# Gate and up products of 32 feed-forward chunks by Strassen's scheme, seven half-size products instead of eight

## The chip, the cores and the metric

The kernel runs on one core of a Trainium2 chip. The metric is the device time of one execution in microseconds (us).

## The reference

`reference()` runs one first block (three mixing branches and an MLP) and then two layers of a second block on x of 512 tokens by 1024 features, all in fp32. Each layer of the second block holds two gated feed-forward blocks with 2816 hidden features, four in all; the change is in these:

```
def swiglu(x, w_gate, w_up, w_down):
    return (jax.nn.silu(x @ w_gate) * (x @ w_up)) @ w_down
...
for l in range(DEPTH_2):
    x = x + 0.5 * swiglu(rms_norm_2(x, ffn1_norm[l]), ffn1_w_gate[l], ffn1_w_up[l], ffn1_w_down[l])
    ...
    x = x + 0.5 * swiglu(rms_norm_2(x, ffn2_norm[l]), ffn2_w_gate[l], ffn2_w_up[l], ffn2_w_down[l])
```

## The kernel before

Activations lie transposed: features on the 128 partitions, the 512 tokens along the free dimension. An fp32 product is made of three TensorE matmuls on fp32r operands (`mm3`, L492): every weight and every activation is kept as a rounded part `_hi` and a remainder `_lo`, and `mm3` adds w_lo x x_hi, w_hi x x_lo and w_hi x x_hi in one PSUM bank.

The weights come as a stream of units of 128x1024 numbers (512 KB) in the order in which TensorE uses them. A unit passes four engines, each with a ring of three slots: SyncE loads it into `raw` when GpSimd has finished the slot's last unit (L408), ScalarE rounds it into `w_hi` (`round_unit`, called by `tick` once TensorE is through with the tile before, two units ahead), GpSimd subtracts in four pieces into `w_lo` (L485), and TensorE waits for `lo_ready` (L500).

A feed-forward block is cut into 11 chunks of 256 hidden features. A chunk is two gate tiles and two up tiles of 128 features by 512 tokens (`project`, 8 x 3 matmuls of 512 columns each, a unit each) and eight down tiles (`down`, 2 x 3 matmuls each, four tiles to a unit). The down tiles of a chunk come after the gate and up tiles of the next one. Gate tiles go to PSUM banks 0 and 1, up and down tiles to a ring of four banks.

The operand of the gate and up tiles is x times the norm's gain; 1/rms of each token (`rt`) is multiplied in afterwards. VectorE scales each gate and up tile by `rt` (L1845, L2273), ScalarE takes silu of the gate, VectorE multiplies gate and up (L2277) and splits the hidden tile (L2240, L2242, in `hidden`), and adds each down tile to the residual `xres` (L2204). In the first block of each layer `layer_columns` (L2409 to L2423) forms some columns for later. Each engine runs its own program; what orders them are the semaphores named in the code.

## Time and profile before

| | |
|---|---|
| median of 3 runs | 3382.36 us (3381.77 to 3383.36) |
| the profiled execution | 3382.04 us, of it 3380.3 us span |
| TensorE | 99% of the span busy, 15438 matmuls |
| VectorE, ScalarE, GpSimd | 50%, 39%, 53% of the span busy |
| granted TensorE clock, mean | 0.999 |

The span runs from the first to the last instruction on the device; the execution's own time has some 1.7 us around it. Busy shares are means over the whole program. Matmuls are pipelined and overlap in the records, so the time of one is read from start to start.

### The profile page before, as it was taken

The numbers are of one execution on the slowest core, as the hardware profiler recorded it, in microseconds if no ns is written. First come the engines' busy times: TensorE is split into PE (matmuls) and PEld (weight loads), VectorE is DVE, ScalarE is ACT, GpSimd is POOL, SyncE is SP. The second block draws the span as 40 slices with busy tenths as digits, with TensorE's granted clock in tenths as the row PEclk, the third lists the DMA queues.
The fourth block names the chain that finished last, engine by engine and source line by source line (L and its number), as shares of the span: only waits on it lengthen the run. The fifth ranks groups of instructions, "written<-read, shape, count | busy, mean of one in ns | idle before, by whom it ended". The sixth has DMA issues, their size and how long they took to land.

```text
span 3380.3 us, 46752 instructions
## 1 busy us (share of the span) xinstructions
PE 3363.0 (99%) x15438; PEld 2740.0 (81%) x15438; DVE 1695.4 (50%) x2673; ACT 1313.9 (39%) x1817; POOL 1801.0 (53%) x2316
## 2 busy tenths in 40 slices
PE   9999999999999999999999999999999999999999
PEld 5888777888888887888888888888887888888887
DVE  8887785544553438614434434544358334243444
ACT  4365664222232226735633222322237545532222
POOL 6444445655555555553455555555556543465554
PEclk9999999999999999999999999999999999999999
DMA  6212552322222323331223222222223222222223
GB/s 224 86 67 69 175 168 100 114 94 99 93 100 94 99 93 101 99 125 63 69 100 102 100 93 99 94 100 93 99 93 112 88 100 75 81 95 98 99 93 112
DMA packets 94459, 343.03 MB, mean 101 GB/s; under 512 B 10609, under 2 KB 11249, under 8 KB 93954
## 3 DMA queue, kind: packets, MB, share of 16 engines
q1 hardware_dynamic: 86978, 312.11, 27.4%
q10 hardware_dynamic: 7360, 29.29, 2.7%
q8 instruction: 78, 1.28, 0.2%
q14 instruction: 43, 0.35, 0.0%
HBM read 335.03 MB, written 2.13 MB: 100 GB/s over the span
## 4 chain that ended last, share of the span: by engine, by line
PE 78%; issue 10%; POOL 7%; DVE 2%; DVEq 1%; ACT 1%; DMA 0%; ACTq 0%; POOLq 0%; SPq 0%
PE ps L494 24%; PE ps L496 24%; PE ps L495 24%; POOL w_lo L485 7%; PE ps L986 1%; PE ps L968 1%; PE ps L660 1%; PE ps L661 1%; PE ps L662 1%; DVE arena L2301 0%; PE ps L977 0%; DVEq L2303 0%; PE ps L626 0%; POOL xres L463 0%; DVE arena L1857 0%
## 5 line engine op out<-in xcount | busy, mean ns | idle before, releaser
L485 POOL TENSOR_TENSOR w_lo<-raw,w_hi 128x256 fp32r<-128x256 f32 x2256 | 1776.6, 818 | 1557.1 <-ACT w_hi L1074 1557.0
L1074 ACT ACTIVATE w_hi<-raw 128x1024 fp32r<-128x1024 f32 x566 | 595.9, 1055 | 1025.9 <-PE ps L496 1007.8
L494 PE MATMUL ps<-a_hi,w_lo 128*128 128x512 f32 x2208 | 873.6, 396 | 0.3 <-DVE a_lo L1803 0.3
L496 PE MATMUL ps<-a_hi,w_hi 128*128 128x512 f32 x2208 | 860.7, 390 | 0.0
L495 PE MATMUL ps<-a_lo,w_hi 128*128 128x512 f32 x2208 | 859.9, 389 | 0.0
L494 PE MATMUL ps<-b_hi,w_lo 128*128 128x512 f32 x2112 | 823.9, 390 | 4.2 <-DVE b_lo L1875 4.0
L495 PE MATMUL ps<-b_lo,w_hi 128*128 128x512 f32 x2112 | 822.5, 389 | 0.0
L496 PE MATMUL ps<-b_hi,w_hi 128*128 128x512 f32 x2112 | 822.4, 389 | 0.0
L494 PEld LDWEIGHTS ps<-a_hi,w_lo 128*128 128x128 f32 x2208 | 414.8, 188 | 100.3 <-issue 16.9
L496 PEld LDWEIGHTS ps<-a_hi,w_hi 128*128 128x128 f32 x2208 | 414.4, 188 | 87.8
L495 PEld LDWEIGHTS ps<-a_lo,w_hi 128*128 128x128 f32 x2208 | 414.9, 188 | 82.6 <-issue 0.5
L494 PEld LDWEIGHTS ps<-b_hi,w_lo 128*128 128x128 f32 x2112 | 396.9, 188 | 89.4 <-issue 6.6
L496 PEld LDWEIGHTS ps<-b_hi,w_hi 128*128 128x128 f32 x2112 | 396.9, 188 | 83.1
L495 PEld LDWEIGHTS ps<-b_lo,w_hi 128*128 128x128 f32 x2112 | 396.8, 188 | 81.6
L2204 DVE SCALAR_TENSOR_TENSOR xres<-ps,xres 128x512 f32<-128x512 f32 x368 | 246.8, 689 | 174.9 <-PE ps L496 165.7
L1845 DVE TENSOR_TENSOR ps<-ps,arena 128x512 f32<-128x512 f32 x96 | 66.3, 699 | 392.0 <-PE ps L496 362.2
L2273 DVE TENSOR_TENSOR ps<-ps,arena 128x512 f32<-128x512 f32 x88 | 61.6, 700 | 282.3 <-PE ps L496 281.9
L1092 ACT ACTIVATE sgate<-ps 128x512 f32<-128x512 f32 x88 | 52.1, 597 | 358.3 <-DVE ps L1845 358.2
L2204 DVE SCALAR_TENSOR_TENSOR xres<-ps,cols,xres 128x512 f32<-128x512 f32 x136 | 99.1, 748 | 65.8 <-PE ps L496 53.7
L2242 DVE TENSOR_TENSOR a_lo<-arena,a_hi 128x512 fp32r<-128x512 f32 x120 | 126.0, 1050 | 9.8 <-issue 1.2
L660 PE MATMUL ps<-w_lo,a_hi 128*128 128x256 f32 x320 | 93.4, 292 | 0.0
L662 PE MATMUL ps<-w_hi,a_hi 128*128 128x256 f32 x320 | 90.4, 283 | 0.0
(286 smaller groups left out, 2772.3 us busy)
## 6 DMA issues: line engine op xcount, KB each, us to landing
raw<-in_stream SPq DMA_DIRECT2D x567, 512.0 KB, 3.3
arena<-in_mod_w ACTq DMA_DIRECT2D x32, 512.0 KB, 4.2
arena<-in_mod_w SPq DMA_DIRECT2D x16, 512.0 KB, 11.5
arena<-arena ACTq DMA_DIRECT2D x16, 256.0 KB, 3.6
arena<-cum_rows ACTq DMA_DIRECT2D x2, 2048.0 KB, 8.0
xres<-in_x_t SPq DMA_DIRECT2D x4, 512.0 KB, 5.1
arena<-in_first SPq DMA_DIRECT2D x8, 256.0 KB, 11.7
xres<-in_x_t ACTq DMA_DIRECT2D x1, 2048.0 KB, 9.5
```

Source lines behind the costliest of these rows:

```text
L485: last = pool.tensor_tensor(w_lo[:, s, part], raw[:, s, part], w_hi[:, s, part].bitcast(F32), ALU.subtract)
L494: pe.matmul(out, lo, x_hi, start=start, stop=False)
L495: pe.matmul(out, hi, x_lo, start=False, stop=False)
L496: return pe.matmul(out, hi, x_hi, start=False, stop=stop)
L660: pe.matmul(out, a_hi[:, f, tok], w_lo[:, s, w], start=f == 0, stop=False)
L662: last = pe.matmul(out, a_hi[:, f, tok], w_hi[:, s, w], start=False, stop=f == KT - 1)
L1074: act.activation(w_hi[:, slot, :], raw[:, slot, :], ACT.Copy).then_inc(hi_ready, 1)
L1092: act.activation(out, ps[:, c.act.n % 2, :], func, bias=bias).then_inc(act_evacuated, 1)
L1845: dve.tensor_tensor(bank, bank, rt, ALU.mult).then_inc(tile_scaled, 1)
L2204: dve.scalar_tensor_tensor(xres[:, m, :], y, scale, xres[:, m, :], ALU.mult, ALU.add).then_inc(dve_evacuated, 1)
L2242: dve.tensor_tensor(a_lo[:, n, :], t, a_hi[:, n, :].bitcast(F32), ALU.subtract).then_inc(hidden_ready, 1)
L2273: dve.tensor_tensor(y, y, rt, ALU.mult)
```

## The change

Of each block's 11 chunks the first three (`PLAIN`) stay as they are, eight (`FAST`) are made anew. In these the gate pair is one product of a 256x1024 weight matrix with 1024x512 activations, cut in halves every way (features out 2 x 128, features in 2 x 512, tokens 2 x 256). Strassen's scheme (in Winograd's form) makes it of seven products of a 128x512 with a 512x256 block instead of eight; each is 4 x 3 matmuls of 256 columns (`fast_product`). The up pair likewise. So a chunk has 14 products, 168 matmuls of 256 columns, in place of 96 of 512. The down tiles are unchanged.

What the scheme adds:

- Activations: once per block, VectorE forms the normalised x (`normalise_x`), its low parts and four combinations of its quarters (`make_turns`), ScalarE rounds them (`round_xn`, `round_turns`), GpSimd makes the combinations' low parts (`low_turns`). All this stands beside the plain chunks 1 and 2. The fast chunks' tiles need no scaling by `rt`.
- Weights: each chunk still loads six units, but rounds and splits nine: VectorE makes four sums of 128x512 for the gate pair and four for the up pair (`sums`), which fill three further units (unit 2: gate, 5: up, 6: both). Units 0 to 2 carry the gate products, 3 to 5 the up products, 6 the last of both, 7 and 8 the down tiles. ScalarE may not round a unit before its sums are written: unit 4 waits for two up sums, units 5 and 6 for all four.
- Results: VectorE joins the products in PSUM by 5 + 2 operations of 128x256 for each pair (`combine`, `combine_last`), after ScalarE has copied the first product aside (`copy_first`).

VectorE's order in a fast chunk is: combine gate, three gate sums for the next chunk, combine up, last combinations, a fourth gate sum, eight down tiles, two hidden tiles, four up sums for the next chunk. SyncE and GpSimd get run lists that change between plain and fast parts.

The diff, cut to its core:

```diff
+PLAIN = 3
+FAST = FFN_CHUNKS - PLAIN
+GROUP, FAST_UNITS, FAST_TILES = 6, 9, 22
+TOK = S // 2
...
+        def fast_raw(part):
+            base = ENDS[part] % RING
+            return fast_own + [raw[:, (base + j) % RING, :] for j in range(3)]
+        def fast_units(part):
+            g1, g2, u1, u2, d1, d2 = fast_raw(part)
+            return [g1, g2, gate_s23, u1, u2, up_s23, both_s4, d1, d2]
...
+                    sp.dma_start(to[j], stream[at + j]).then_inc(fast_loaded[j], 16)
+                with sp.Fori(1, FAST) as i:
+                    for j, unit in enumerate((2, 2, 5, 5, 7, 8)):
+                        sp.wait_ge(fast_lo, i * FAST_UNITS + (done - FAST_UNITS + unit + 1))
+                        sp.dma_start(to[j], stream[bass.ds(i * GROUP + (at + j), 1)].rearrange("o p n -> p (o n)")
+                                     ).then_inc(fast_loaded[j], 16)
...
+                with pool.Fori(0, FAST) as i:
+                    for j, of in enumerate(fast_units(part)):
+                        s = (end + j) % RING
+                        pool.wait_ge(fast_hi, i * FAST_UNITS + (part * FAST * FAST_UNITS + j + 1))
+                        low(w_lo[:, s, :], of, w_hi[:, s, :]).then_inc(fast_lo, 1)
...
+            def fast_product(out, j, half, operand):
+                pe.wait_ge(fast_lo, c.fast_lo.at(j + 1))
+                s = (c.units.n + j) % RING
+                for k in range(4):
+                    w = slice(half * 4 * P + k * P, half * 4 * P + k * P + P)
+                    x_hi, x_lo = operand(k)
+                    last = mm3(out, w_hi[:, s, w], w_lo[:, s, w], x_hi, x_lo, k == 0, k == 3)
+                last.then_inc(fast_done, 1)
...
+                    fast_product(ps[:, x, left], j, 0, x_1a)
+                    free(-2, -3)
+                    fast_product(ps[:, z, left], j, 1, x_2a)
+                    free(-1, -1)
+                    fast_product(ps[:, y, right], j + 1, 0, t_1)
+                    fast_product(ps[:, y, left], j + 1, 1, t_4)
+                    fast_product(ps[:, z, right], j + 2, 0, t_2)
+                    free(0, 0)
+                    fast_product(ps[:, w, left], j + 2, 1, t_3)
+                for half, banks in enumerate((gate_banks, UP_BANKS)):
+                    pe.wait_ge(first_copied, c.gate_silu.at(1 + half))
+                    fast_product(ps[:, banks[0], right], 6, half, x_2b)
+                pe.wait_ge(hidden_ready, c.hid.at(2))
...
+            def fast_round(j, chunk):
+                raw_at = {0: 0, 1: 1, 3: 2, 4: 3, 7: 4, 8: 5}
+                if j in raw_at:
+                    act.wait_ge(fast_loaded[raw_at[j]], c.fast_raw.at(16 * chunk + 16))
+                if j in (1, 2, 6):
+                    act.wait_ge(gate_summed, c.gate_sums.at(4 * chunk + {1: 2, 2: 4, 6: 4}[j]))
+                if j in (4, 5, 6):
+                    act.wait_ge(up_summed, c.up_sums.at(4 * chunk + {4: 2, 5: 4, 6: 4}[j]))
+                slot = (ENDS[c.part.n] + j) % RING
+                act.activation(w_hi[:, slot, :], fast_units(c.part.n)[j], ACT.Copy).then_inc(fast_hi, 1)
+            def fast_silu(m):
+                bank = fast_banks(c.part.n)[2 * m]
+                act.wait_ge(gate_ready, c.gate_ready.at(2 - m))
+                act.activation(sgate[:, m, :], ps[:, bank, :], ACT.Silu).then_inc(gate_silu, 1)
+                table[0] = "evicted"
+            def copy_first(bank, to):
+                act.activation(to, ps[:, bank, 0:TOK], ACT.Copy).then_inc(first_copied, 1)
+            def fast_chunk(last):
+                for j in range(3, FAST_UNITS):
+                    act.wait_ge(fast_done, c.fast.at(2 * (j - 2)))
+                    fast_round(j, 0)
+                    if j == 4:
+                        act.wait_ge(hidden_ready, c.hid.at(0))
+                        copy_first(fast_banks(c.part.n)[0], gate_m1)
+                    if j == 6:
+                        fast_silu(1)
+                        copy_first(UP_BANKS[0], up_m1)
+                fast_silu(0)
+                for j, tiles in enumerate((14, 18, 22)):
+                    act.wait_ge(fast_done, c.fast.at(tiles))
+                    if not last:
...
+                def first_chunk(m):
+                    round_xn(2 * m)
+                    round_xn(2 * m + 1)
+                gate_tiles(True, first_chunk)
...
+                gate_tiles(True, lambda m: round_turns(1 + m))
+                tick()
+                round_turns(3)
...
+            def normalise_x(g, k):
+                for i in range(2):
+                    last = dve.scalar_tensor_tensor(x_turns[k][:, i * S:i * S + S], xres[:, 4 * i + k, :], par(PAR2, g, 4 * i + k), rt,
+                                                    ALU.mult, ALU.mult)
+                last.then_inc(xn_ready, 1)
+            def make_turns(k):
+                x_1a, x_1b, x_2a, x_2b = (x_turns[k][:, i * TOK:i * TOK + TOK] for i in range(4))
+                dve.wait_ge(xn_rounded, 4 * c.part.n + k + 1)
+                dve.tensor_tensor(q11_lo[:, k, :], x_1a, q11_hi[:, k, :].bitcast(F32), ALU.subtract)
+                dve.tensor_tensor(a_lo[:, 4 + k, :], x_turns[k][:, S:2 * S], a_hi[:, 4 + k, :].bitcast(F32), ALU.subtract)
+                dve.drain()
+                dve.tensor_tensor(x_1a, x_1b, x_1a, ALU.subtract)
+                dve.drain()
+                dve.tensor_tensor(x_1b, x_2b, x_1b, ALU.subtract)
+                dve.drain()
+                dve.tensor_tensor(x_2b, x_2b, x_1a, ALU.subtract)
+                dve.drain()
+                dve.tensor_tensor(x_2a, x_2a, x_2b, ALU.subtract).then_inc(turns_made, 1)
+            def sums(kind, first, end, chunk):
+                gate = kind == "gate"
+                raws = fast_raw(c.part.n)
+                one, two = raws[0:2] if gate else raws[2:4]
+                s23, s4 = (gate_s23, both_s4[:, 0:S]) if gate else (up_s23, both_s4[:, S:2 * S])
+                summed = gate_summed if gate else up_summed
+                for n in range(first, end):
+                    dve.drain()
+                    if n == 0:
+                        for j in (0, 1) if gate else (2, 3):
+                            dve.wait_ge(fast_loaded[j], c.fast_raw.at(16 * chunk + 16))
+                        if chunk:
+                            dve.wait_ge(fast_lo, c.fast_lo.at(3 if gate else 6))
+                        dve.tensor_tensor(s23[:, S:2 * S], one[:, 0:S], two[:, 0:S], ALU.subtract).then_inc(summed, 1)
+                    if n == 1:
+                        dve.tensor_tensor(two[:, 0:S], two[:, 0:S], two[:, S:2 * S], ALU.add).then_inc(summed, 1)
+                    if n == 2:
+                        dve.tensor_tensor(s23[:, 0:S], two[:, 0:S], one[:, 0:S], ALU.subtract).then_inc(summed, 1)
+                    if n == 3:
+                        if chunk:
+                            dve.wait_ge(fast_lo, c.fast_lo.at(7))
+                        dve.tensor_tensor(s4, one[:, S:2 * S], s23[:, 0:S], ALU.subtract).then_inc(summed, 1)
...
+            def combine(banks, tiles, copied, m1, u4):
+                x, z, y, w = blocks(banks)
+                dve.wait_ge(first_copied, c.gate_silu.at(copied))
+                dve.wait_ge(fast_done, c.fast.at(tiles))
+                dve.tensor_tensor(sum_u2, m1, z[1], ALU.add)
+                dve.drain()
+                dve.tensor_tensor(sum_u3, sum_u2, w[0], ALU.add)
+                dve.tensor_tensor(u4, sum_u2, y[1], ALU.add)
+                dve.drain()
+                dve.tensor_tensor(y[0], sum_u3, y[0], ALU.add)
+                return dve.tensor_tensor(y[1], sum_u3, y[1], ALU.add)
...
+            def combine_last(banks, tiles, m1, u4):
+                x, z = blocks(banks)[0:2]
+                dve.drain()
+                dve.wait_ge(fast_done, c.fast.at(tiles))
+                dve.tensor_tensor(x[0], m1, z[0], ALU.add)
+                return dve.tensor_tensor(x[1], u4, x[1], ALU.add)
...
+            def fast_hidden(half, m):
+                if m == 0:
+                    dve.wait_ge(gate_silu, c.gate_silu.at(2))
+                t = tt[:, m, :]
+                dve.tensor_tensor(t, sgate[:, m, :], ps[:, UP_BANKS[2 * m], :], ALU.mult).then_inc(up_read, 1)
+                hidden(half, m, t)
+            def fast_chunk(last):
+                gate_banks = fast_banks(c.part.n)
+                assert (c.dve.n + c.dve.shift) % WIDE == FAST_BANK[c.part.n]
+                combine(gate_banks, 6, 1, gate_m1, gate_u4).then_inc(gate_ready, 1)
+                if not last:
+                    sums("gate", 0, 3, 1)
+                combine(UP_BANKS, 12, 2, up_m1, up_u4)
+                combine_last(gate_banks, 13, gate_m1, gate_u4).then_inc(gate_ready, 1)
+                combine_last(UP_BANKS, 14, up_m1, up_u4)
+                if not last:
+                    sums("gate", 3, 4, 1)
+                for m in range(8):
+                    fast_down(m)
+                    if last and m in (1, 4):
                         dve.drain()
-                        add_tiles(ffn_out)
+                        fast_hidden(1, m // 4)
...
+            def ffn_chunks(g):
+                def first_beside(n):
+                    if n == 0:
+                        normalise_x(g, 2)
+                        normalise_x(g, 3)
+                    if n == 1:
+                        make_turns(0)
+                normalise_x(g, 0)
+                normalise_x(g, 1)
+                ffn_up(1, first_beside)
+                dve.drain()
+                add_tiles(ffn_out)
+                make_turns(1)
+                def second_beside(n):
+                    if n < 2:
+                        make_turns(2 + n)
+                    if n == 2:
+                        dve.wait_ge(turns_ready, 4 * c.part.n + 1)
+                        sums("gate", 0, 2, 0)
+                    if n == 3:
+                        sums("gate", 2, 3, 0)
+                ffn_up(0, second_beside)
+                dve.drain()
+                add_tiles(ffn_out)
                 dve.memset(cols[:, 126:127], 0.0).then_inc(normalised, 1)
...
+                dve.drain()
+                with loop(dve, FAST - 1, c, fast=FAST_TILES, fast_raw=16, fast_lo=FAST_UNITS, gate_silu=2):
+                    fast_chunk(False)
+                fast_chunk(True)
```

Where the order of instructions changes: the first place is VectorE at the end of a chunk. Before, in a turn of its loop, a hidden tile follows its up tile; `arena` in the first row is `rt`.

```order
L2273 TENSOR_TENSOR ps<-ps,arena 128x512 [waits tiles_done]
L2275 ISA
L2277 TENSOR_TENSOR arena<-sgate,ps 128x512 [waits act_evacuated]
L2240 CAST a_hi<-arena 128x512
L2242 TENSOR_TENSOR a_lo<-arena,a_hi 128x512
```

Now, with the last down tile in the first row; `arena` and `raw` in L2634 to L2642 are weight units and their sums.

```order
L2673 SCALAR_TENSOR_TENSOR xres<-ps,xres 128x512 [waits fast_done]
L2680 TENSOR_TENSOR arena<-sgate,ps 128x512 [waits gate_silu]
L2555 CAST a_hi<-arena 128x512
L2557 TENSOR_TENSOR a_lo<-arena,a_hi 128x512
L2680 TENSOR_TENSOR arena<-sgate,ps 128x512
L2555 CAST a_hi<-arena 128x512
L2557 TENSOR_TENSOR a_lo<-arena,a_hi 128x512
L2633 REGISTER_ALU [waits fast_loaded3,fast_loaded2]
L2634 TENSOR_TENSOR arena<-arena,raw 128x512 [waits fast_lo]
L2636 TENSOR_TENSOR raw<-raw 128x512
L2638 TENSOR_TENSOR arena<-raw,arena 128x512
L2642 TENSOR_TENSOR arena<-arena 128x512 [waits fast_lo]
```

The two hidden tiles have moved behind all eight down tiles, and four sums, each with both inputs in SBUF, stand behind them.

The second place is ScalarE in a fast chunk, from the rounding of unit 3 on. Before, a rounding waited for a load and a tile alone:

```order
L1073 REGISTER_ALU [waits tiles_done]
L1074 ACTIVATE w_hi<-raw 128x1024 [waits raw_loaded0]
L1091 REGISTER_ALU [waits dve_evacuated]
L1092 ACTIVATE sgate<-ps 128x512 [waits tile_scaled]
L187 REGISTER_ALU
L1074 ACTIVATE w_hi<-raw 128x1024 [waits raw_loaded1,tiles_done]
L187 REGISTER_ALU
L1074 ACTIVATE w_hi<-raw 128x1024 [waits raw_loaded2,tiles_done]
```

Now:

```order
L1785 ACTIVATE w_hi<-arena 128x1024 [waits fast_loaded2]
L1800 REGISTER_ALU
L1783 ISA [waits fast_loaded3,fast_done]
L1785 ACTIVATE w_hi<-raw 128x1024 [waits up_summed]
L1803 ISA
L1795 ACTIVATE arena<-ps 128x256 [waits hidden_ready]
L1800 REGISTER_ALU
L1783 REGISTER_ALU [waits fast_done]
L1785 ACTIVATE w_hi<-arena 128x1024 [waits up_summed]
L1800 REGISTER_ALU
L1785 ACTIVATE w_hi<-arena 128x1024 [waits up_summed,gate_summed,fast_done]
```

The second, third and fourth rounding (units 4, 5 and 6) now wait for VectorE's sums, and every later rounding stands behind them in ScalarE's queue.

## Rows read from the trace of the kernel before

**Rows 1.** The page: busy us (share of span) x instructions; costliest groups.
```profile
PE 3363.0 (99%) x15438; PEld 2740.0 (81%) x15438; DVE 1695.4 (50%) x2673; ACT 1313.9 (39%) x1817; POOL 1801.0 (53%) x2316
...
L485 POOL TENSOR_TENSOR w_lo<-raw,w_hi 128x256 fp32r<-128x256 f32 x2256 | 1776.6, 818 | 1557.1 <-ACT w_hi L1074 1557.0
```

**Rows 2.** Windows of 100 us in a feed-forward block.
```profile
core 0: us, PE busy (x) PEld busy (x) DVE busy (x) ACT busy (x) POOL busy (x), PEclk, DMA share, GB/s
1900.00:2000.00 100.00, 100.00 (x443) 82.83 (x442) 38.74 (x55) 22.02 (x24) 56.70 (x75) 1.00 0.28 95
2000.00:2100.00 100.00, 100.00 (x443) 82.84 (x442) 39.16 (x56) 23.07 (x25) 54.72 (x73) 1.00 0.29 97
```

**Rows 3.** Timeline of TensorE there: start us, us, engine line op.
```profile
2000.41 0.39 PE L496 MATMUL ps<-b_hi,w_hi 128*128 128x512 f32 x1
2000.64 0.39 PE L494 MATMUL ps<-a_hi,w_lo 128*128 128x512 f32 x1
```

**Rows 4.** Timeline of VectorE there; in brackets idle time and who ended it.
```profile
2000.84 0.70 DVE L2273 TENSOR_TENSOR ps<-ps,arena 128x512 f32<-128x512 f32 x1 [2.13 <-PE ps L496]
2001.69 0.69 DVE L2277 TENSOR_TENSOR arena<-sgate,ps 128x512 f32<-128x512 f32 x1
2002.46 0.53 DVE L2240 CAST a_hi<-arena 128x512 fp32r<-128x512 f32 x1
2003.07 1.07 DVE L2242 TENSOR_TENSOR a_lo<-arena,a_hi 128x512 fp32r<-128x512 f32 x1
...
2017.16 0.70 DVE L1845 TENSOR_TENSOR ps<-ps,arena 128x512 f32<-128x512 f32 x1 [4.75 <-PE ps L496]
2022.60 0.70 DVE L1845 TENSOR_TENSOR ps<-ps,arena 128x512 f32<-128x512 f32 x1 [4.74 <-PE ps L496]
```

**Rows 5.** Timeline of GpSimd there.
```profile
2001.98 3.47 POOL L485 TENSOR_TENSOR w_lo<-raw,w_hi 128x256 fp32r<-128x256 f32 x4 [1.98 <-ACT w_hi L1074]
2007.50 2.83 POOL L485 TENSOR_TENSOR w_lo<-raw,w_hi 128x256 fp32r<-128x256 f32 x4 [2.05 <-ACT w_hi L1074]
2012.94 2.82 POOL L485 TENSOR_TENSOR w_lo<-raw,w_hi 128x256 fp32r<-128x256 f32 x4 [2.61 <-ACT w_hi L1074]
```

**Rows 6.** Timeline of TensorE in the first block, matmuls of 256 columns.
```profile
157.43 0.28 PE L660 MATMUL ps<-w_lo,a_hi 128*128 128x256 f32 x1
...
159.83 0.28 PE L662 MATMUL ps<-w_hi,a_hi 128*128 128x256 f32 x1
```

**Rows 7.** Groups of VectorE by shape, whole span: busy us, mean ns, idle before.
```profile
L2164 DVE SCALAR_TENSOR_TENSOR arena<-ps,arena 128x256 f32<-128x256 f32 x8 | 3.4, 425 | 2.2 <-ACT arena L1368 1.6
```

**Rows 8.** Two lines of VectorE, whole span: ns min/median/max of one.
```profile
L2204 DVE SCALAR_TENSOR_TENSOR xres<-ps,xres x368: 676/691/694, 977.5 to 3377.1; 128x512 f32<-128x512 f32 x184
...
L2242 DVE TENSOR_TENSOR a_lo<-arena,a_hi x120: 692/1069/1073, 593.0 to 3357.6; 128x512 fp32r<-128x512 f32 x120
```

**Rows 9.** Timelines of GpSimd and VectorE where both are dense.
```profile
2532.89 8.84 POOL L485 TENSOR_TENSOR w_lo<-raw,w_hi 128x256 fp32r<-128x256 f32 x8 [2.30 <-ACT w_hi L1074]
...
2532.36 6.47 DVE L2301 SCALAR_TENSOR_TENSOR arena<-arena,params 128x512 f32<-128x512 f32 x6
2538.75 1.22 DVE L1857 SCALAR_TENSOR_TENSOR arena<-xres,params,arena 128x512 f32<-128x512 f32 x1
2539.90 1.22 DVE L1803 TENSOR_TENSOR a_lo<-arena,a_hi 128x512 fp32r<-128x512 f32 x1
```

**Rows 10.** Timeline of ScalarE in the feed-forward block.
```profile
2000.84 1.06 ACT L1074 ACTIVATE w_hi<-raw 128x1024 fp32r<-128x1024 f32 x1 [4.38 <-PE ps L496]
```

**Rows 11.** Timeline of TensorE at its one wait for GpSimd.
```profile
591.37 0.39 PE L496 MATMUL ps<-b_hi,w_hi 128*128 128x512 f32 x1
591.92 0.50 PE L494 MATMUL ps<-b_hi,w_lo 128*128 128x512 f32 x1 [0.16 <-POOL w_lo L485]
592.25 0.39 PE L495 MATMUL ps<-b_lo,w_hi 128*128 128x512 f32 x1
```

**Rows 12.** Timeline of VectorE at the head of the first feed-forward block.
```profile
952.17 0.70 DVE L2273 TENSOR_TENSOR ps<-ps,arena 128x512 f32<-128x512 f32 x1 [2.08 <-PE ps L496]
...
954.48 1.07 DVE L2242 TENSOR_TENSOR a_lo<-arena,a_hi 128x512 fp32r<-128x512 f32 x1
...
958.43 0.16 DVE L2423 TENSOR_SCALAR cols<-cols 128x8 f32<-128x8 f32 x1
```

**Rows 13.** The page, DMA issues: KB each, us to landing.
```profile
raw<-in_stream SPq DMA_DIRECT2D x567, 512.0 KB, 3.3
```

More of the change, by code:

```diff
@@ new lines, in low_run @@
+            def low_run(first, end):
+                n = first
+                while n < end:
+                    turns = (end - n) // RING
+                    if n % RING == 0 and turns:
+                        with pool.Fori(n // RING, n // RING + turns) as i:
+                            for s in range(RING):
+                                pool.wait_ge(hi_ready, i * RING + (s + 1))
+                                low(w_lo[:, s, :], raw[:, s, :], w_hi[:, s, :]).then_inc(lo_ready, 1)
+                        n += turns * RING
+                    else:
+                        s = n % RING
+                        pool.wait_ge(hi_ready, n + 1)
+                        low(w_lo[:, s, :], raw[:, s, :], w_hi[:, s, :]).then_inc(lo_ready, 1)
+                        n += 1
@@ L910, in ffn @@
                 project(bank_v(), of=OF_B)
-                with loop(pe, FFN_CHUNKS // 2, c, units=12, tiles=24, act=4, dve=20, hid=4):
+                for chunk in range(1, PLAIN):
                     up()
-                    down(0)
-                    up()
-                    down(1)
-                down(0)
-                c.dve.ring = 2
+                    down((chunk - 1) % 2)
+                c.part.n += 1
+                pe.wait_ge(turns_ready, 4 * c.part.n)
+                fast_chunk(True)
```

269 lines of the change are left out of this document (231 added, 38 removed).

## The prediction, made before the changed kernel ran

> **What bounds the kernel now.** I read the page first: TensorE has work in 99% of the span, GpSimd in 53% [rows 1]. The windows of 100 us inside a feed-forward block then show TensorE at 100%, 443 matmuls in each, clock granted in full, VectorE at 39%, ScalarE at 22%, GpSimd at 57% [rows 2]. The timeline of TensorE shows a new 512-column matmul every 0.227 us and no wait between tiles [rows 3]. VectorE's scaling of one tile and of the next start 5.44 us apart, which is 24 matmuls of 0.2267 us, and it is idle before them, waiting for TensorE [rows 4]. GpSimd takes 2.82 us for a weight unit and then sits idle about 2 us until ScalarE has rounded the next one [rows 5]. So TensorE's stream of columns is the bound, and the others wait for it. A chunk costs 144 matmuls, 144 x 0.2267 = 32.64 us.
>
> **The half-size products.** The trace has this shape: in the first block, 256-column matmuls start at 157.43 and at 159.83 us with 19 between, 0.120 us apart [rows 6]. A unit of 1024 weight columns feeds two products of 12 such matmuls, 24 x 0.120 = 2.88 us. A fast chunk is then seven units of 2.88 (20.16 us) and two down units of 24 x 0.2267 = 5.44 us (10.88), 31.04 us in all. Against 32.64 that is 1.60 us less, and 32 such chunks (8 in each of 4 blocks) would give 51 us back, if TensorE stays the bound. The Trainium skill ("TensorE: Matmul & The Clock Gate", section on the gap between matmuls) gives N/2.4 ns plus 2.5 ns, 109 ns for 256 columns. The row has 120, and 227 where the rule has 216, so the measurement decides. By the rule's 109 ns TensorE's seven units would be 1.8 us shorter per chunk, 58 us more over 32 chunks, if nothing else bound.
>
> **What the others must do for it.** A fast chunk has 9 units to round and to split instead of 6: three are weight sums that VectorE writes. GpSimd needs 9 x 2.82 = 25.4 us per 31.04 us, where it needed 16.9 per 32.64. VectorE makes 8 sums of 128x512 with both inputs in SBUF, and 14 combinations of 128x256 with one input in PSUM. The nearest row for the latter is 0.425 us [rows 7]. It loses the four scalings of 0.70 us.
>
> The two engines do not run such work side by side. Where VectorE has one PSUM input its time does not move (L2204: 676 to 694 ns), but the subtraction of two SBUF tiles, L2242, spreads from 692 to 1073 ns [rows 8]. On the same stretch the GpSimd unit beside one cast and one such subtraction took 3.47 us instead of 2.82 [rows 4, 5]. Where both are dense, eight GpSimd instructions took 8.84 us instead of 2 x 2.82 = 5.64, while VectorE's two-SBUF operations took 1.08 to 1.22 us each [rows 9]: each such operation costs GpSimd 3.20/8 = 0.40 us and itself about 0.38. The Trainium skill ("SBUF — State Buffer", who interferes with whom) states that a VectorE instruction with two SBUF inputs and a GpSimd one that reads SBUF exclude each other for the whole instruction. The rows agree, and this rule speaks against the change. In total GpSimd would need 25.4 + 8 x 0.40 + 2 x 0.65 = 29.9 us of 31.04: not the bound by its sum. But the weight ring has three slots, so it cannot work ahead, and what counts is the order inside the chunk.
>
> **One fast chunk, walked.** Time 0 is TensorE's end of a chunk's eighth down tile; unit k of the next chunk is due at 2.88k.
> - VectorE starts 0.20 after a tile ends (2000.64 to 2000.84, [rows 3, 4]), and adds the tile in 0.69 [rows 8]: 0.89.
> - Two hidden tiles (product, cast, subtraction), 2001.69 to 2004.14 = 2.45 each [rows 4], with some 0.1 between: 6.0. Before the change nothing near waited for this.
> - The first two up sums, at 1.07 plus 0.08 for the drain each, as L2242 has it beside GpSimd [rows 4]: 8.3. ScalarE's rounding of unit 4 waits for them (L1783 to L1785), and units 5 to 8 stand behind it in its queue.
> - ScalarE 1.06, GpSimd 0.08 behind it [rows 5, 10]: GpSimd starts unit 4 at 9.5. Beside it run the last sums, one of them in full: 2.82 + 0.40, done at 12.7. TensorE wanted it at 11.52.
> - VectorE is through the up sums at 10.6, combines the gate products (5 operations of about 0.42, L2653 to L2659) to 12.7 and goes into three sums for the next chunk. Beside them GpSimd's unit 5 takes 2.82 + 3 x 0.40 = 4.0: done at 16.75.
> - TensorE restarts 0.1 to 0.2 late: after its one wait for GpSimd the next matmul starts 0.33 behind the first instead of 0.227 [rows 11]. It starts unit 5 at 16.9, where 5 x 2.88 = 14.40 was due.
>
> Behind that point GpSimd keeps up: units 6 to 8 see VectorE on PSUM inputs, and the two down units are 10.88 us long. So a chunk lasts 31.04 + 2.5 = 33.5 us. Register operations ahead of waits are not in the walk (the gap between L2273 and L2277 is 0.15 where a drain alone leaves 0.08, [rows 4]), and I take 33.7. That is 1.06 more than 32.64, and 34 us over 32 chunks. The first and the last chunk of a block go much the same: in the first, unit 2 waits for a gate sum that now stands behind the last additions (some 1.2 us), in the last, the hidden tiles lie between the additions.
>
> **Entry of each block.** Normalising x (8 operations), the 16 differences and 8 low parts go beside plain chunks 1 and 2, which have the time (VectorE 39% busy). In the two blocks where VectorE also forms per-layer columns (954.48 + 1.07 to 958.6, [rows 12]), ScalarE's second tick of plain chunk 1 stands behind two normalised tiles. From chunk 1's start at 951.97 (the scaling at 952.17 less 0.20): columns done 6.6, four normalisings at 1.1 to 11.1, ScalarE's rest to 12.7, rounding to 13.8, GpSimd 2.82 + 4 x 0.40 to 18.3, and TensorE wants that unit at 3 x 5.44 = 16.3. I add 2 us for each of these two blocks, 4 in all; nothing for the other two, where it comes 3.1 us earlier. The turned inputs' low parts (16 GpSimd instructions, 11.3 us per block) lie in its 45% of idle time. Loads: 6 units a chunk as before, 3.3 us from issue to landing [rows 13], and each is asked for more than 5 us ahead: nothing. If a load came late, its whole lateness would reach TensorE.
>
> **Sum.** The profiled execution took 3382.0 us (3380.3 span and 1.7 around it), the median 3382.4. 3382 + 34 + 4 = 3420 us, 1.1% slower.
>
> **Rivals.**
> - *The port costs nothing on the path, faster.* If sums and units pass each other, unit 5 is on time, the chunk lasts 31.04, and 3382 - 51 + 4 = 3335 us. It decides at 16.0 us in the walk: 0.9 less than I have makes the chunk as long as before. For it: GpSimd's sum of 29.9 us fits. Against it: four two-SBUF operations stand in a row ahead of unit 4, and I have read their price twice. Chance 0.18, with all that ends between. A further 0.06 for a chunk at 32.64 within 0.2 us.
> - *GpSimd stays behind, slower still.* If units 6 to 8 too take 3.3 us, 0.4 above the 2.88 of TensorE, 1.2 us more a chunk: 3420 + 38 = 3458 us. For it: at unit 5 there is no idle time of GpSimd left. Against: its neighbours on VectorE then have PSUM inputs. Chance 0.12.
> - *The entry stalls in all four blocks*, about 8 us each where I have 1 on average: 3448 us. VectorE's extra work there is some 31 us in 65 (20 wide two-SBUF operations at 1.1, 20 of 256 columns at about 0.45). Chance 0.04.
>
> **How the numbers follow.** Forecast 0.60. Its own range is 3395 to 3445: a contended operation at 0.35 or 0.45 us instead of 0.40, and 0.3 us of waits per chunk either way. Bounds: an up sum at 0.69 (no contention) or 1.22 (the longest row), so 2 x 0.38 less or 2 x 0.15 more; combinations at 0.3 or 0.6. The range 3360 to 3460 reaches into the first rival and takes in the second. A measurement tells about 0.2% (7 us) from no change: faster 0.18, same 0.06, slower 0.76.
>
> **What would show it.** In a window in the fast part: TensorE below 100%, its idle time ended by w_lo on GpSimd ahead of 256-column matmuls, two or three times a chunk, the longest ahead of units 4 and 5; a chunk of 33.7 us; GpSimd near 90%; sums near 1.1 us, combinations near 0.4; ScalarE waiting for VectorE's raw sum ahead of unit 4. A chunk of 31.1 us, or GpSimd units at 2.9 us beside the sums, would make me wrong; so would 256-column matmuls that do not start 0.120 us apart, or waits for a DMA.

## The result and the profile after

The changed kernel takes 3443.4 us, median of four runs from 3439.3 to 3455.5, against 3382.5 us: ratio 1.0186, interval 1.016 to 1.0212. It is 61 us slower. The profiled execution was the fastest of the four, 3439.31 us with a span of 3437.6, against 3382.04 and 3380.3 before. The runs are now 16 us apart; before the change they were 1.6 us apart.

The page's busy line, and two groups of its costliest:

```profile
PE 3337.1 (97%) x17742; PEld 2805.1 (82%) x17742; DVE 2158.1 (63%) x3377; ACT 1466.4 (43%) x2025; POOL 2221.6 (65%) x2764
...
L634 PE MATMUL ps<-a_hi,w_lo 128*128 128x512 f32 (+1 forms) x2720 | 1023.1, 376 | 21.7 <-DVE xres L2673 14.2
...
L588 POOL TENSOR_TENSOR w_lo<-arena,w_hi 128x256 fp32r<-128x256 f32 x768 | 642.2, 869 | 124.7 <-ACT w_hi L1785 124.7
```

The windows that answer to [rows 2], now filled with fast chunks:

```profile
1900.00:2000.00 100.00, 91.73 (x626) 83.99 (x625) 68.23 (x101) 32.88 (x39) 84.56 (x105) 0.98 0.27 95
2000.00:2100.00 100.00, 93.68 (x643) 85.85 (x642) 71.80 (x108) 33.00 (x39) 87.61 (x107) 1.00 0.25 90
```

TensorE idles 6 to 8% of a stretch in which it never idled before. Its timeline in one fast chunk, which began at 1119.69 us, cut to the rows with a wait in brackets:

```profile
1128.94 0.39 PE L634 MATMUL ps<-q_hi,w_lo 128*128 128x256 f32 x1 [0.59 <-POOL w_lo L588]
1132.80 0.39 PE L634 MATMUL ps<-t_hi,w_lo 128*128 128x256 f32 x1 [0.74 <-POOL w_lo L588]
1136.47 0.39 PE L634 MATMUL ps<-t_hi,w_lo 128*128 128x256 f32 x1 [0.59 <-POOL w_lo L588]
```

These are the first matmuls of units 3, 4 and 5, at 9.25, 13.11 and 16.78 us of the chunk, where 8.64, 11.52 and 14.40 were due. Each waits for GpSimd's low part. VectorE and GpSimd in that chunk:

```profile
1126.25 0.90 DVE L2634 TENSOR_TENSOR arena<-arena,raw 128x512 f32<-128x512 f32 x1 [0.25 <-issue]
1127.25 1.06 DVE L2636 TENSOR_TENSOR raw<-raw 128x512 f32<-128x512 f32 x1
1128.40 1.04 DVE L2638 TENSOR_TENSOR arena<-raw,arena 128x512 f32<-128x512 f32 x1
```

```profile
1129.48 3.27 POOL L588 TENSOR_TENSOR w_lo<-raw,w_hi 128x256 fp32r<-128x256 f32 x4 [0.59 <-ACT w_hi L1785]
1132.70 6.96 POOL L588 TENSOR_TENSOR w_lo<-arena,w_hi 128x256 fp32r<-128x256 f32 x8
```

A sum takes 1.04 to 1.06 us beside GpSimd, and the eight GpSimd instructions of units 5 and 6 take 6.96 us instead of 2 x 2.82 [rows 5]. Inner fast chunks follow each other at 33.89 us (median of the starts of unit 0; a plain chunk is 32.64).

Two chunks of the first block, one of the second and one of the fourth are 2.3 to 3.9 us longer still. VectorE in one of them:

```profile
1211.02 0.42 DVE L2667 TENSOR_TENSOR ps<-arena,ps 128x256 f32<-128x256 f32 x1
1211.59 4.76 DVE L2642 TENSOR_TENSOR arena<-arena 128x512 f32<-128x512 f32 x1
1216.27 2.47 DVE L2673 SCALAR_TENSOR_TENSOR xres<-ps,xres 128x512 f32<-128x512 f32 x4
```

GpSimd and TensorE at the same place:

```profile
1207.41 5.62 POOL L588 TENSOR_TENSOR w_lo<-raw,w_hi 128x256 fp32r<-128x256 f32 x8
1212.97 2.82 POOL L588 TENSOR_TENSOR w_lo<-arena,w_hi 128x256 fp32r<-128x256 f32 x4
1217.36 2.81 POOL L588 TENSOR_TENSOR w_lo<-arena,w_hi 128x256 fp32r<-128x256 f32 x4 [1.56 <-ACT w_hi L1785]
```

```profile
1218.28 0.49 PE L634 MATMUL ps<-a_hi,w_lo 128*128 128x512 f32 x1 [2.17 <-DVE xres L2673]
```

The fourth gate sum (L2642), elsewhere 1.23 us, takes 4.76: it is done only after GpSimd's unbroken run has ended at 1215.79. GpSimd's twelve instructions from 1207.41 on take their undisturbed 0.70 us each. Four additions of down tiles queue behind the sum, and TensorE, which wants their banks, stands still for 2.17 us. I call this a shut-out. The trace has four (L2642 at 1211.6, 1248.0, 1923.7 and 3173.6).

**Where the 57.3 us of span went**, from the starts of TensorE's units: inner chunks 24 x 1.25 = 30.0; the first fast chunk of each block 4 x (33.39 - 32.64) = 3.0; the last 4 x (34.51 - 32.64) = 7.5; shut-outs 11.2 (two of 2.48, one of 3.93, one of 2.34); the rest is 5.6, of which some 5.4 are the entries of the blocks.

### The profile page after: what moved, and what is told of

It reads as the page before. It is cut to its first block, busy times and chain, and to the rows that moved or that the text cites. A ratio compares the mean times of both kernels' runs of the same rounds, so it can differ in the third digit from the quotient of the medians.

```text
span 3437.6 us, 53314 instructions
## 1 busy us (share of the span) xinstructions
PE 3337.1 (97%) x17742; PEld 2805.1 (82%) x17742; DVE 2158.1 (63%) x3377; ACT 1466.4 (43%) x2025; POOL 2221.6 (65%) x2764
## 4 chain that ended last, share of the span: by engine, by line
POOL 41%; PE 31%; issue 22%; DVE 3%; ACT 2%; DVEq 1%; POOLq 0%; ACTq 0%; DMA 0%; SPq 0%
POOL w_lo L588 39%; PE ps L634 8%; PE ps L636 8%; PE ps L635 8%; POOL t_lo L588 1%; PE ps L1217 1%; PE ps L1199 1%; PE ps L801 1%; PE ps L802 1%; PE ps L803 1%; DVE arena L2761 0%; PE ps L1208 0%; DVEq L2763 0%; ACT w_hi L1305 0%; DVE arena L2172 0%
## 5 line engine op out<-in xcount | busy, mean ns | idle before, releaser
L634 PE MATMUL ps<-a_hi,w_lo 128*128 128x512 f32 (+1 forms) x2720 | 1023.1, 376 | 21.7 <-DVE xres L2673 14.2
L636 PE MATMUL ps<-a_hi,w_hi 128*128 128x512 f32 (+1 forms) x2720 | 1006.1, 370 | 0.0
L635 PE MATMUL ps<-a_lo,w_hi 128*128 128x512 f32 (+1 forms) x2720 | 1005.6, 370 | 0.0
L588 POOL TENSOR_TENSOR w_lo<-arena,w_hi 128x256 fp32r<-128x256 f32 x768 | 642.2, 869 | 124.7 <-ACT w_hi L1785 124.7
L634 PE MATMUL ps<-b_hi,w_lo 128*128 128x512 f32 x1088 | 425.9, 391 | 4.7 <-DVE b_lo L2190 4.0
L635 PE MATMUL ps<-b_lo,w_hi 128*128 128x512 f32 x1088 | 424.0, 390 | 0.0
L636 PE MATMUL ps<-b_hi,w_hi 128*128 128x512 f32 x1088 | 423.9, 390 | 0.0
L634 PE MATMUL ps<-t_hi,w_lo 128*128 128x256 f32 x1024 | 292.8, 286 | 44.1 <-POOL w_lo L588 44.1
L636 PE MATMUL ps<-t_hi,w_hi 128*128 128x256 f32 x1024 | 286.9, 280 | 0.0
L635 PE MATMUL ps<-t_lo,w_hi 128*128 128x256 f32 x1024 | 285.4, 279 | 0.0
```

Source lines behind the costliest of these rows:

```text
L588: last = pool.tensor_tensor(to[:, at], of[:, at], hi[:, at].bitcast(F32), ALU.subtract)
L634: pe.matmul(out, lo, x_hi, start=start, stop=False)
L635: pe.matmul(out, hi, x_lo, start=False, stop=False)
L636: return pe.matmul(out, hi, x_hi, start=False, stop=stop)
```

## The experiments

VectorE's instructions in a fast chunk are written below as sg0 to sg3 (gate sums), su0 to su3 (up sums), cg, cu (combinations), lg, lu (last combinations), d0 to d7 (additions of down tiles), h0, h1 (hidden tiles). The changed kernel has `cg sg0 sg1 sg2 cu lg lu sg3 d0..d7 h0 h1 su0..su3`. Kernels 1, 2 and 8 were run once, the others four to ten times.

**1. Sums with one input.** The eight sums become copies of 128x512, so the weights' sums are left out. With the second input the instruction changes too: TENSOR_REDUCE in place of TENSOR_TENSOR.

```diff
+            def one_input(to, of):
+                one = lambda v: v.rearrange("p (n o) -> p n o", o=1)
+                return dve.tensor_reduce(to, one(of), mybir.AxisListType.X, ALU.add)
-                        dve.tensor_tensor(s23[:, S:2 * S], one[:, 0:S], two[:, 0:S], ALU.subtract).then_inc(summed, 1)
+                        one_input(s23[:, S:2 * S], one[:, 0:S]).then_inc(summed, 1)
```

> All eight weight sums of a fast chunk are written by an operation of the same 512 columns with one SBUF input instead of two (the sums' values are wrong by this, so the result is not the reference's). Theory A, VectorE's two-input operations and GpSimd exclude each other: the sums take 0.6 to 0.7 us each, GpSimd's units beside them 2.8 us, unit 4 is late by 0.3 us and unit 5 not at all, a chunk lasts 31.3 us and the run 3347 us. Theory B, what counts is that the up sums stand behind the hidden tiles in VectorE's order: only the sums' own time shrinks, 0.38 us for each of two on the path, a chunk lasts 33.1 us and the run about 3410 us. Theory C, a ring of three slots cannot carry nine units per chunk whatever VectorE does: the chunk stays at 33.9 us and the run near 3440 us.

Measured: 3354.6 us, inner chunks of 31.57 us. VectorE's timeline there, three sums in one row, and GpSimd's beside them:

```profile
1187.85 2.24 DVE L2623 TENSOR_REDUCE arena<-arena 128x512 f32<-128x512 f32 x3 [0.33 <-issue]
```

```profile
1187.14 5.62 POOL L588 TENSOR_TENSOR w_lo<-arena,w_hi 128x256 fp32r<-128x256 f32 x8
```

The same number of instructions of the same width, at the same places, no longer lengthen GpSimd's: 5.62 us for the eight that took 6.96. What the two-input sums do to GpSimd costs 2.3 us in an inner chunk, and with it go the shut-outs: 3443.4 - 3354.6 = 89 us. The chunk did not reach the 31.3 us that were expected: unit 4 is still some 0.5 us late.

**2. Sums of 8 columns.** All but 8 columns of each sum are left out; the second input stays.

```diff
-                        dve.tensor_tensor(s4, one[:, S:2 * S], s23[:, 0:S], ALU.subtract).then_inc(summed, 1)
+                        dve.tensor_tensor(s4[:, 0:8], one[:, S:S + 8], s23[:, 0:8], ALU.subtract).then_inc(summed, 1)
```

> The eight sums shrink to 8 columns each (their other values stay unwritten, so the result is not the reference's); all waits and all nine units stay. Theory A: only the hidden tiles contend with GpSimd, TensorE never waits for a weight unit, a chunk lasts 31.04 us, the run 3340 us. Theory B: the path loses the sums, also about 31 us. Theory C: the chunk stays at 33.9 us, the run near 3440 us. Together with the run with one input per sum it parts the time that the sums take from what they cost through the port: A expects the two runs within 0.3 us per chunk.

Measured: 3394.1 us, far off all that was expected. The trace says why:

```profile
1138.26 3.91 DVE L2642 TENSOR_TENSOR arena<-arena 128x8 f32<-128x8 f32 x1
```

A sum of 8 columns took 3.91 us, and it did so in 27 of 28 chunks, each time ending with GpSimd's run. So the length is not the sum's own, and my first idea of the shut-out, a coin toss when a sum and a GpSimd instruction start together, fell too: this one began 0.3 us into a GpSimd instruction.

**3. Only the fourth gate sum moved**, behind d3, where GpSimd has been idle.

> Only the fourth gate sum moves, from ahead of the first down tile to behind the fourth, where GpSimd has idle time. In the changed kernel it took 4.1 to 4.8 us in four chunks of the profiled run instead of 1.3. Theory A, it is shut out by GpSimd's unbroken run of instructions by chance: no sum over 1.4 us is left, every inner chunk lasts 33.8 to 33.9 us, the run 3428 us, and the runs agree within 3 us (the changed kernel's lie 16 us apart). Rival: sums are shut out wherever GpSimd is busy: long sums come up again in other chunks, and the runs still differ by 10 us or more around 3440 us.

Measured: 3438.1 us (3427.1 to 3448.4), ratio 1.0176 (1.0158 to 1.0195). The profiled run is the one at 3427.1, and in it no sum took over 1.3 us. But the four runs lie 21 us apart, as the rival had it, and not within 3. The other three have no trace. Their mean granted clock is 0.997 to 0.998 where the traced run has 1.000, so TensorE ran at its lower level somewhere in them; what held it up is open.

**4. An order made for the 0.4 us price**: `sg0 cg cu lg sg1 sg2 sg3 d0 d1 d2 su0 d3 d4 su1 d5 su2 su3 d6 d7 lu h0 h1`.

> The same operations in another order on VectorE, inner fast chunks only: first gate sum, combine gate, combine up, last gate combination, three gate sums, then the eight down tiles with the four up sums between them (one behind the third and the fifth, two behind the sixth), last up combination, hidden tiles. Nothing is left out. Theory A: the up sums are done before the chunk ends, unit 4 no longer waits for them, and no unit meets more than one or two two-input operations: a chunk lasts 31.04 to 31.3 us, the run 3346 us, 1.1% faster than before the change. Theory B, order alone: the same direction. Theory C: the chunk stays at 33.9 us. Rival: two-input operations between the down tiles make VectorE late for the down banks, TensorE waits there, a chunk lasts 32.5 us or more and the run 3385 us or more.

Measured: 3513.4 us, ratio 1.0392 (1.0375 to 1.0409), 167 us from the forecast. The second gate sum was shut out in 26 of 28 chunks:

```profile
1154.42 5.39 DVE L2636 TENSOR_TENSOR arena<-arena 128x512 f32<-128x512 f32 x1
```

**What the traces have in common.** For each VectorE instruction with two SBUF inputs that started beside a GpSimd instruction I counted how many GpSimd had by then finished without a break, a break being idle time or an instruction that VectorE had lengthened, and how many more started before the VectorE instruction ended. Over the TENSOR_TENSOR instructions of the ten traces of the changed kernel with full-width sums, those below included: of 5,608 with a count up to 7, none had to let more than two pass. Of 110 with a count of 8 to 11, 11 had to let four or more pass. Of 55 with a count of 12 to 14, 48 did (four of the other seven met the end of GpSimd's run, three got in behind one). Another 25 had a longer run behind them: 24 met its end within two, one got in behind one. Hence the theory of the next four: a long unbroken run of GpSimd shuts VectorE out, and a break ends it. The break is made by a `drain`, one more instruction in GpSimd's program that computes nothing.

**5. The changed kernel with four GpSimd drains in a chunk.**

```diff
                         s = (end + j) % RING
+                        if j in (0, 6, 7, 8):
+                            pool.drain()
                         pool.wait_ge(fast_hi, i * FAST_UNITS + (part * FAST * FAST_UNITS + j + 1))
```

> The changed kernel with a GpSimd drain ahead of units 0, 6, 7 and 8 of each fast chunk, so that GpSimd's instructions can't overlap there; nothing else changes. Theory A: a VectorE sum is shut out only where GpSimd has run about eight or more instructions unbroken since it last idled or VectorE last broke in (in the traces so far: none of some 2,200 with seven or fewer, all that had really thirteen or more), and a drain breaks the run. Then no fourth gate sum takes over 2 us, inner chunks stay at 33.9 us, all runs lie within 5 us of each other, and the time is 3427 us (3440 less the four or five shut-outs of 2.5 to 3 us), up to 3432 for what the drains cost GpSimd. Rival B: the shut-out has to do with the sum's place behind the last combinations, or with what VectorE did before: then sums of over 4 us remain, the runs spread over 10 us and more, and the median stays at 3438 to 3445.

Measured: 3437.5 us, all four runs from 3437.3 to 3438.3, ratio 1.0165 (1.0148 to 1.0182). One sum of a first chunk was still shut out (3.35 us), none of an inner one, and the spread shrank from 16 us to 1. The drains cost more than was expected: inner chunks are 34.09 us, 0.20 longer, since GpSimd is what is late.

**6. The order of 4 with the same drains.**

> The order of e3_order (up sums between the down tiles, first gate sum ahead of the first combination, the other gate sums together) with the same four drains on GpSimd. e3_order took 3513.4 us with one sum shut out for 5.4 us in 26 of 28 chunks and inner chunks of 36.8 to 37.6 us. Theory A: the drains end the shut-outs; what is left is each sum's 0.4 us of GpSimd, now where GpSimd has time: inner chunks of 31.1 to 32.0 us, 3350 to 3370 us, below the kernel before. Rival B: shut-outs stay, 3500 us or more. Rival C: no shut-outs, but the spacing of sums between down tiles makes down banks late by itself: 33 us for a chunk and over, 3400 us and more.

Measured: 3377.5 us (3377.2 to 3378.2, ten runs), ratio 0.9986 (0.9976 to 0.9996). Same VectorE order as 3513.4 us; four drains took off 136 us. Inner chunks 32.00 us, no sum over 1.3 us. The rivals fell, the one of 4 too: with the shut-outs gone the sums between the down tiles cost no more than this. The kernel stayed 8 us above the expected band, in places that 9 and 11 take up.

**7. Another order, no drain**: `cg sg0 sg1 cu lg lu d0 d1 sg2 d2 d3 su0 sg3 d4 su1 d5 su2 d6 su3 d7 h0 h1`.

> Another order and no drain: combination, gate sums 0 and 1, the other combinations, down tiles 0 and 1, gate sum 2, tiles 2 and 3, up sum 0, gate sum 3, tile 4, up sum 1, tile 5, up sum 2, tile 6, up sum 3, tile 7, hidden tiles. Every sum behind a down tile meets GpSimd when it is idle or newly started. Theory A (shut-out after about eight unbroken instructions, 0.4 us of GpSimd for a sum that meets it): no sum over 2 us, inner chunks of 32 to 32.6 us, 3365 to 3385 us. Rival B (the price of a sum is the same wherever it stands): inner chunks stay at 33.9 us and the time at 3425 to 3440 us.

Measured: 3400.9 us (3400.7 to 3401.0), ratio 1.0055 (1.0039 to 1.0072), inner chunks 33.00 us. It is 42 us better than the changed kernel, so the place of a sum matters, and rival B fell. But I had misjudged GpSimd's idle time behind d1:

```profile
1176.43 2.10 DVE L2638 TENSOR_TENSOR arena<-arena 128x512 f32<-128x512 f32 x1
```

GpSimd's run was fourteen or fifteen instructions old here and had two to go; the sum waited for both, in all 28 chunks, and TensorE waited 31.4 us in total for the additions behind it.

**8. Sums of 8 columns with the drains.**

> e2_no_sums (sums of 8 columns for 512) with the four drains. It leaves out the sums, as e2 does. e2 took 3394.1 us, with the fourth gate sum, of 8 columns, shut out for 3.5 to 3.9 us in 27 of 28 chunks and inner chunks of 33.1 us. Theory A: without the shut-outs inner chunks are 31.1 to 31.3 us and the time 3338 to 3345 us, what was expected of e2. Rival B: 3390 us and more.

Measured: 3354.4 us. The drains took 40 us off kernel 2, but it did not reach 3345 (one 8-column sum, in a first chunk, still took 2.53 us): inner chunks are 31.61 us, with TensorE 0.35 us late at unit 4. Even an 8-column sum beside GpSimd took about 0.61 us where it takes 0.17 alone: it waits for the running instruction to end.

**9, 10. One drain, the entry and the last chunk**, on kernel 6; the second with the drain at unit 8.

```diff
-                        if j in (0, 6, 7, 8):
+                        if j == 7:
...
-                    if n == 3:
-                        sums("gate", 2, 3, 0)
...
-                add_tiles(ffn_out)
+                add_tiles(ffn_out[:4])
+                sums("gate", 2, 3, 0)
+                add_tiles(ffn_out[4:5])
+                dve.wait_ge(turns_ready, 4 * c.part.n + 3)
+                sums("gate", 3, 4, 0)
+                add_tiles(ffn_out[5:])
...
+                    dve.drain()
+                    fast_hidden(1, 0)
                     for m in range(8):
                         fast_down(m)
-                        if m in (1, 4):
+                        if m == 3:
                             dve.drain()
-                            fast_hidden(1, m // 4)
+                            fast_hidden(1, 1)
```

> e8_order_drains (3377.5 us) with three more edits. One drain, ahead of unit 7, for four: the second gate sum then meets GpSimd four or five instructions after a break. Entry: gate sum 2 goes behind the fourth addition of the last plain chunk, gate sum 3 behind the fifth, instead of ahead of the first and behind the last. Last fast chunk of a block: its hidden tiles ahead of the first down tile and behind the fourth, instead of behind the second and the fifth. Theory A: the drains gave up some 0.3 us in a chunk (inner chunks 31.6 to 31.9 us instead of 32.0), the entry gives back 0.8 us ahead of the first fast chunk and 1.5 us of the wait at 7.1 us in it, four times, and the last chunk's wait of 1.9 us falls to 0.5 us, four times: 3377.5 - 7 - 9 - 6 = 3355 us, between 3350 and 3364. Rival B: these waits are not VectorE's order but the sum of its work, and come back behind: 3370 us and more. Rival C: one drain is too few and shut-outs return: over 3380 us, with sums of over 4 us in the trace.

> As e11_entry_and_last, but the drain stands ahead of unit 8 instead of unit 7, right where the second gate sum comes. If a drain only has to lie within eight instructions of the sum, the time is that of e11_entry_and_last within 3 us. If a sum has to be lucky to fall behind it, shut-outs of 4 to 5 us return in some chunks and the time is 10 us or more above it.

Measured: 3364.1 us (ratio 0.995, 0.9936 to 0.9963) and 3364.7 us (0.9947, 0.9932 to 0.9963). The drain's place makes no difference to the median, as the theory has it. One of the first kernel's five runs took 3370.1 us, the others 3363.5 to 3364.6; it has no trace. The forecast of 3355 us was 9 us short. The last chunk fell from 32.91 to 31.48 us and the wait ahead of the first fast chunk is gone, as expected. Inner chunks are 31.88 us. But the wait at 7.1 us in the first fast chunk stayed, 1.27 us from start to start in place of 1.59, and with it most of the 6 us that I had counted for it. I had taken ScalarE's rounding of unit 2 to be held back by the gate sum; with the sum done at 1016.7 us it still starts at 1020.63, on a tile of TensorE:

```profile
1020.63 1.06 ACT L1787 ACTIVATE w_hi<-arena 128x1024 fp32r<-128x1024 f32 x1 [1.88 <-PE ps L638]
```

**11. The first up sum behind d3** instead of ahead of it, on kernel 9.

> As e11_entry_and_last, but the first up sum stands behind the addition of down tile 3 instead of ahead of it. In e8_order_drains that addition came 0.4 us late for TensorE (gap of 0.54 us at 27.8 us of the chunk). Theory A: the gap goes, 0.4 us in each of 28 chunks: up to 11 us faster than e11_entry_and_last, unless the up sums, later by 0.7 us, delay unit 4. Rival: they do, and the time is the same or above.

Measured: 3349.3 us (3348.7 to 3349.8), ratio 0.9902 (0.9886 to 0.9917). Inner chunks fell from 31.88 to 31.33 us. This version beats both kernels. Its windows of fast chunks, to be read beside the two above, and its VectorE behind the last combinations (the kernel's lines are two further down):

```profile
1900.00:2000.00 100.00, 99.67 (x676) 91.91 (x675) 73.77 (x117) 34.42 (x40) 93.03 (x116) 1.00 0.29 100
2000.00:2100.00 100.00, 99.67 (x695) 92.67 (x694) 73.92 (x117) 35.52 (x41) 91.29 (x115) 1.00 0.27 94
```

```profile
1165.55 0.42 DVE L2669 TENSOR_TENSOR ps<-arena,ps 128x256 f32<-128x256 f32 x1
1166.07 0.80 DVE L2638 TENSOR_TENSOR arena<-arena 128x512 f32<-128x512 f32 x1
1166.95 1.05 DVE L2640 TENSOR_TENSOR arena<-arena 128x512 f32<-128x512 f32 x1
```

GpSimd there, where the drain ahead of unit 7 shows as 0.23 us without work (in 31 of the 32 fast chunks):

```profile
1156.92 5.63 POOL L588 TENSOR_TENSOR w_lo<-arena,w_hi 128x256 fp32r<-128x256 f32 x8
1162.78 6.97 POOL L588 TENSOR_TENSOR w_lo<-raw,w_hi 128x256 fp32r<-128x256 f32 x8 [0.23 <-issue]
```

GpSimd is at 91 to 93% and TensorE waits 0.3% of the time: the sums' 0.4 us are all still paid, beside units that TensorE does not want yet. In the block starts: inner chunks 24 x (31.33 - 32.64) = -31.4, last ones 4 x (31.49 - 32.64) = -4.6, first ones 4 x (33.02 - 32.64) = +1.5, together -34.5; the medians are 33.1 us apart, and the rest lies at the entries.

**12. The same without its drain.**

> e13_up_sum_later (3349.3 us) without its one GpSimd drain; the order of VectorE's instructions is untouched. Theory A: the drain is what keeps the second gate sum from being shut out; without it GpSimd has run some twelve to fourteen instructions unbroken when that sum comes, as in e3_order, the sum waits 4 to 5.5 us in nearly all of 28 chunks and each costs 4.5 to 5.5 us: 3475 to 3500 us. Rival B: e3_order was slow for its last chunks or its first up sum, and the drain only tidies: 3345 to 3360 us.

Measured: 3515.1 us (3510.1 to 3520.5), ratio 1.0387 (1.037 to 1.0405). One GpSimd drain in a chunk is worth 166 us; the time is 15 us above the band I gave. TensorE's lower clock behind the waits adds up to 2.8 us to a chunk, and 11 us come from a place that I had not counted, the last chunks (below). The same sum, GpSimd beside it, and TensorE behind it:

```profile
1148.16 5.43 DVE L2636 TENSOR_TENSOR arena<-arena 128x512 f32<-128x512 f32 x1
1153.68 0.69 DVE L2638 TENSOR_TENSOR arena<-arena 128x512 f32<-128x512 f32 x1
```

```profile
1139.07 5.62 POOL L588 TENSOR_TENSOR w_lo<-arena,w_hi 128x256 fp32r<-128x256 f32 x8
1144.62 5.65 POOL L588 TENSOR_TENSOR w_lo<-raw,w_hi 128x256 fp32r<-128x256 f32 x8
1150.20 2.84 POOL L588 TENSOR_TENSOR w_lo<-arena,w_hi 128x256 fp32r<-128x256 f32 x4
```

```profile
1157.15 0.79 PE L634 MATMUL ps<-a_hi,w_lo 128*128 128x512 f32 x1 [3.79 <-DVE xres L2673]
1157.74 0.63 PE L635 MATMUL ps<-a_lo,w_hi 128*128 128x512 f32 x1
1158.17 0.63 PE L636 MATMUL ps<-a_hi,w_hi 128*128 128x512 f32 x1
...
1162.74 0.39 PE L635 MATMUL ps<-a_lo,w_hi 128*128 128x512 f32 x1
```

The sum waits from 1148.16 to the end of GpSimd's run at 1153.04. TensorE then idles 3.79 us, and starts again 0.43 us apart instead of 0.227, for twelve matmuls: another 2.4 us.

Three of the four last chunks, which have no sums, are 3.6 us longer too. What was shut out there has one SBUF input, the CAST of a hidden tile, elsewhere 0.43 to 1.1 us:

```profile
1299.97 3.42 DVE L2555 CAST a_hi<-arena 128x512 fp32r<-128x512 f32 x1
```

```profile
1294.71 8.40 POOL L588 TENSOR_TENSOR w_lo<-raw,w_hi 128x256 fp32r<-128x256 f32 x12
```

It too ends behind GpSimd's run, which ended at 1303.11. So the number of inputs does not by itself say which instructions are at risk.

## Why the prediction was right, and where its sizes were off

The change was forecast to add 38 us and added 61. The mechanism on the path was the one forecast, but the median lies only 1.6 us inside the upper bound of 3445, and two of the four runs lie outside. The range was drawn for other uncertainties than the shut-outs; that it still held the median was partly luck.

- **TensorE's own pace** held: 31.04 us a chunk. Kernel 11 comes within 0.3 us of it.
- **The port** held, and is shown by kernel 1: GpSimd pays 0.40 to 0.45 us for each two-input sum (1.34 us for three in the rows above). The Trainium skill ("SBUF — State Buffer", section on the two separate sides) has the pair of ports that the two engines share locked for a whole instruction; kernel 8 agrees, where 8 columns cost as long as the GpSimd instruction under way.
- **The walk** held to 0.15 us at its end: GpSimd late at unit 4, TensorE at unit 5 at 16.78 us where 16.9 was forecast. Two errors offset each other on the way: unit 4 starts at 13.11 us, some 0.3 later than the walk has it, and unit 5 follows it by 3.67, where the walk has 4.0 for GpSimd. Not foreseen was that unit 3 is late too. The chunk lasted 33.89 us where I had taken 33.7. That makes 24 x 0.19 = 4.6 us more on the inner chunks.
- **"The first and the last chunk of a block go much the same"** failed for the last: its hidden tiles, between the additions, hold TensorE for 1.84 us ahead of a down tile, and it lasts 34.51 us. The first took 33.39. Together with the inner ones 40.5 us where the sum has 34. Kernel 9 shows the cause by moving the hidden tiles (the last chunk is 1.43 us shorter, the inner ones, which share only the change of drains, 0.12).
- **The entry** was put in two blocks, at ScalarE's tick, with 4 us. It is some 5.4 us and lies in all four: about 1.1 us each ahead of the first fast chunk, and 0.45 us more at the tick in the two blocks where I had put it. So the term came out near for a reason that it did not contain. Ahead of the first fast chunk a gate sum stands before the additions of the last plain one:

```profile
1012.98 0.47 PE L634 MATMUL ps<-a_hi,w_lo 128*128 128x512 f32 x1 [0.86 <-DVE xres L2519]
```

  With the sum moved behind the additions (kernel 9) that wait is gone.
- **The step that is missing** is the shut-out: "each such operation costs GpSimd 0.40 us and itself about 0.38" has no term for a sum that does not get in. It is 11.2 us of the profiled run, and makes the other runs unlike each other (kernel 5 takes the spread away). The price itself was near for a sum that gets in.
- Summed up: 40.5 - 34 = 6.5 for the chunks, 11.2 for shut-outs and 5.6 - 4 = 1.6 for the entry and the small rest make 3420 + 19.3 = 3439.3, the profiled run.
- **The rivals.** That GpSimd stays behind at units 6 to 8 did not come: TensorE is 0.3 us late at unit 6 and not behind it. The port rival would have given 3335 us with the order as it is; kernels 1 and 8 show that this is not to be had there, and kernel 11 that it nearly is in another order. That the entry stalls in all four blocks came true, but with 1.1 to 1.6 us each in place of 8.

What stays open: why a long run shuts VectorE out and a short one does not (the counts give the condition, not the mechanism), why a CAST with one SBUF input was held too, and the spread of kernel 3.

## What to carry to other kernels

Where VectorE has instructions with two SBUF inputs, or a CAST as in kernel 12, and GpSimd runs without a break, look for their longest time, not their mean: a long one ends where GpSimd's run ends, and what is queued behind it pays. A GpSimd drain within about seven instructions ahead of such an operation can be worth several us and costs some 0.05 us, an estimate from kernel 5 (0.20 for four). Then place these operations where GpSimd's output is not wanted next: the sums of kernel 11 cost GpSimd as much as before, and TensorE hardly waits.

## What the runs showed of the hardware that was not expected

- A VectorE TENSOR_TENSOR with two SBUF inputs got in within two GpSimd instructions in all 5,608 cases with up to seven finished GpSimd instructions behind a break (about 5 us), and had to let four or more pass in 48 of 55 with twelve to fourteen. Its width does not matter for this (8 columns: 3.91 us; 512 columns: 5.43 us). A CAST with one SBUF input was held for 3.42 us in the same way, three times in kernel 12.
- The Trainium skill ("SBUF — State Buffer", section on the two separate sides) says that who starts first holds the shared ports for the whole instruction. That is one instruction's wait, 0.70 us here; the traces show waits over six and seven of them.
- After 2.04 us of waiting TensorE's matmuls in the changed kernel started 0.43 us apart until 1933.7, and the window gives the clock there as 0.57 of full speed, the lower level of 1.2 GHz for most of it:

```profile
1930.00:1934.00 4.00, 4.00 (x12) 3.11 (x11) 0.92 (x2) 0.00 (x0) 1.69 (x3) 0.57 0.00 0
```

  After the other three shut-outs, with waits of much the same length, the matmuls kept their pace. In kernel 4 24 of 27 such waits, and in kernel 12 29 of 30, most of about 3.8 us, were followed by five to twelve matmuls 0.43 us apart; their mean clock is 0.981 and 0.977.
